# A fused two-block network on one core: the sums of the later modulation vectors streamed through columns of ones, two vectors at a time

## The reference

```python
cond = jax.nn.silu(c)                                   # (1, 1024)
for i in range(2):
    mod = (cond @ ada_w[i] + ada_b[i])[:, None, :]       # (1, 1, 6144)
    sh1, sc1, g1, sh2, sc2, g2 = jnp.split(mod, 6, axis=-1)
    h = rmsnorm(x, norm1_g[i]) * (1.0 + sc1) + sh1
    y = attention_i(h)                                   # 0: sliding window with sinks, 1: stick breaking
    x = x + g1 * y
    h = rmsnorm(x, norm2_g[i]) * (1.0 + sc2) + sh2
    x = x + g2 * swiglu(h, w_gate[i], w_up[i], w_down[i])
# then one hybrid mixer (gated convolution and SSD scan), a convolutional MLP, a last rmsnorm
```

## Time and profile before

| | us |
|---|---|
| median of 3 runs | 2310.65 (2310.07 to 2312.83) |
| the profiled execution | 2311.6 |
| its span, first to last instruction | 2309.8 |
| TensorE busy in the span | 2261.5 |
| DVE busy | 1168.9 |
| ACT busy | 883.7 |

### The profile page before, as it was taken

One profiled execution on the slowest core, in us unless ns is written; L12 is line 12 of the kernel. 1 busy time (PEld: TensorE's weight loads), 2 busy tenths in 40 slices (PEclk: granted clock), 3 DMA queues, 4 the chain that ended last, 5 costly groups with the idle time before them and its releaser, 6 DMA issues.

```text
span 2309.8 us, 27339 instructions
## 1 busy us (share of the span) xinstructions
PE 2261.5 (98%) x11136; PEld 1823.2 (79%) x11136; DVE 1168.9 (51%) x1619; ACT 883.7 (38%) x1422; POOL 165.0 (7%) x145
## 2 busy tenths in 40 slices
PE   7999999999999999999999999999999999999998
PEld 4777788888767677888887878887788887888886
DVE  4764755543455654333335446467753345553453
ACT  3654322232354543222233226467653223332331
POOL 2112000000100010000001001032120001000001
PEclk9999999999999999999999999999999999999999
DMA  9332555622212122222222223433223232323322
GB/s 343 129 108 93 190 214 199 218 101 96 78 66 72 46 74 82 99 93 100 93 99 82 100 92 111 138 105 117 98 92 128 92 101 82 100 83 109 101 82 83
DMA packets 82173, 259.13 MB, mean 112 GB/s; under 512 B 8800, under 2 KB 17248, under 8 KB 82048
## 3 DMA queue, kind: packets, MB, share of 16 engines
q1 hardware_dynamic: 82048, 257.38, 32.2%
HBM read 253.09 MB, written 4.26 MB: 111 GB/s over the span
## 4 chain that ended last, share of the span: by engine, by line
PE 93%; DVE 3%; ACT 1%; issue 1%; POOL 1%; DMA 0%; DVEq 0%; POOLq 0%; SPq 0%; ACTq 0%
PE pb L803 27%; PE pb L807 27%; PE pb L805 27%; PE pb L1015 1%; PE pb L1040 1%; PE pb L1025 1%; PE pb L848 1%; PE pb L1100 1%; PE pb L823 1%; PE pb L897 1%; PE pb L827 1%; PE pb L825 1%; PE pb L991 1%; DVE slab L1720 1%; PE pb L1106 0%
## 5 line engine op out<-in xcount | busy, mean ns | idle before, releaser
L803 PE MATMUL pb<-hhi,whi 128*128 128x512 f32 x1976 | 783.2, 396 | 4.6 <-ACT hhi L1185 3.0
L805 PE MATMUL pb<-hhi,wlo 128*128 128x512 f32 x1976 | 770.2, 390 | 2.3 <-DVE wlo L1449 2.3
L807 PE MATMUL pb<-hlo,whi 128*128 128x512 f32 x1976 | 771.0, 390 | 0.0
L1449 DVE TENSOR_TENSOR wlo<-raw,whi 128x1024 fp32r<-128x1024 f32 x361 | 447.7, 1245 | 570.0 <-ACT whi L1157 569.8
L1157 ACT ACTIVATE whi<-raw 128x1024 fp32r<-128x1024 f32 x361 | 380.2, 1057 | 730.7 <-PE pb L807 711.8
L803 PEld LDWEIGHTS pb<-hhi,whi 128*128 128x128 f32 x1976 | 370.7, 188 | 92.1 <-issue 17.8
L805 PEld LDWEIGHTS pb<-hhi,wlo 128*128 128x128 f32 x1976 | 371.1, 188 | 80.8 <-DVE wlo L1449 3.1
L807 PEld LDWEIGHTS pb<-hlo,whi 128*128 128x128 f32 x1976 | 370.6, 188 | 80.9 <-DVE hlo L1524 1.1
L803 PE MATMUL pb<-ahi,whi 128*128 128x512 f32 x848 | 334.9, 395 | 1.4 <-ACT ahi L1336 0.7
L807 PE MATMUL pb<-alo,whi 128*128 128x512 f32 x848 | 330.9, 390 | 0.0
L805 PE MATMUL pb<-ahi,wlo 128*128 128x512 f32 x848 | 330.5, 390 | 0.0
(11 more groups left out here) (234 smaller groups left out, 1676.1 us busy)
## 6 DMA issues: line engine op xcount, KB each, us to landing
raw<-stream SPq DMA_DIRECT2D x361, 512.0 KB, 3.2
slab<-ada_w SPq DMA_DIRECT2D x80, 512.0 KB, 4.8
early<-ada_w SPq DMA_DIRECT2D x32, 256.0 KB, 8.1
slab<-sums SPq DMA_DIRECT2D x32, 256.0 KB, 4.1
X<-xT SPq DMA_DIRECT2D x8, 256.0 KB, 4.9
ya<-slab SPq DMA_DIRECT2D x8, 256.0 KB, 3.5
slab<-ya SPq DMA_DIRECT2D x8, 256.0 KB, 5.1
outT<-X SPq DMA_DIRECT2D x8, 256.0 KB, 2.1
```

Source lines behind the costliest of these rows:

```text
L803: e.matmul(out, wh, hi, start=s.k == 0, stop=False)
L805: e.matmul(out, wl, hi, start=False, stop=False)
L807: i = e.matmul(out, wh, lo, start=False, stop=s.last)
L1449: e.tensor_tensor(wlo[:, u % NW, :], raw[:, u % NRAW, :], whi[:, u % NW, :].bitcast(F), ALU.subtract).then_inc(*v_cut.up(u))
```

## The change

The column sums of an accumulator go the other way round. A column of ones, repeated to 32 columns, is the stationary side, and the accumulator streams through it in two halves of 512, each into 32 partitions of one bank. Two accumulators (js) can stand side by side, in 64 partitions each. ACT copies the bank to SBUF (`modrows`), TensorE turns four pieces of up to 128 columns (`modturn`), and DVE takes one column of each 32 and adds the bias (`modadd`). Copy, turn and add come 4, 8 and 10 products behind the sums. There are six such groups instead of ten blocks: (2), (3,4), (5), (6,7), (8,9), (10,11). The group of j = 3 moves to where j = 4 stood; the pairs of the FFN stand one step behind the last accumulation of the pair, in a step of their own; (10,11) stands inside the FFN.

```diff
+    def column_sums(*js):
+        tick("modsum", js)
+        s.soon(3, "modrows", js)
+        s.soon(7, "modturn", js)
+        s.soon(9, "modadd", js)
+
     def mods():
         for j in range(2, 12):
             for k in range(KD):
-                if k == 3 and j not in (2, 5):
-                    tick("modsum", j - 1)
+                if k == 3 and j in (3, 6):
+                    column_sums(j - 1)
                 tick("fma", 8 * j + k)
                 yield 1
+            if j in (7, 9, 11):
+                column_sums(j - 1, j)
+                yield 1
...
         run(woven(some(steps, 8), some_mods(2), 3))
-        tick("modsum", 4)
+        column_sums(3, 4)
         run(steps)
...
     ffn(0, 1)
-    run(mod)
-    tick("modsum", 11)
+    assert next(mod, None) is None
...
-        def modsum(j):
-            l, jj = MODS[j]
-            b = take(("mod", j))
-            w.wait_ge(d_in, "vec")
-            w.wait_ge(v_mod, ("fma", 8 * j + 7))
-            for d in range(8):
-                i = e.matmul(b[:, d:d + 1], modacc[j % 2][:, quarter(d)], C("one"), start=d == 0, stop=True, skip_group_check=True)
-            i.then_inc(*t_mod.up(j))
-            give(("mod", j), v_mod, ("add", j))
+        def modsum(js):
+            b = take(("mod", js))
+            for n, j in enumerate(js):
+                w.wait_ge(v_mod, ("fma", 8 * j + 7))
+                for half in range(2):
+                    g = 64 * n + 32 * half
+                    i = e.matmul(b[g:g + 32, :], C("one").to_broadcast([P, 32]), modacc[j % 2][:, S * half:S * half + S], start=True, stop=True,
+                                 skip_group_check=True)
+            i.then_inc(*t_mod.up(*js))
+            give(("mod", js), a_att, ("modrows", js))
+
+        def modturn(js):
+            b = take(("columns", js))
+            n = slice(0, 64 * len(js))
+            w.wait_ge(a_att, ("modrows", js))
+            for d in range(4):
+                i = e.transpose(b[:, P * d:P * d + 64 * len(js)], sums_at(js)[n, quarter(d)], ident[n, n])
+            i.then_inc(*t_mod.up(("columns", js)))
+            give(("columns", js), v_mod, ("add", js[-1]))
...
+    def sums_at(js):
+        return slot(46) if js[-1] <= 4 else slot(16)
...
+        def modrows(js):
+            n = slice(0, 64 * len(js))
+            w.wait_ge(t_mod, js[-1])
+            e.activation(sums_at(js)[n, :], bank(("mod", js))[n, :], ACT.Copy).then_inc(*a_att.up(("modrows", js)))
...
-        def modsum(j):
+        def modadd(js):
+            for n, j in enumerate(js):
+                add_bias(js, n, j)
+
+        def add_bias(js, n, j):
             l, jj = MODS[j]
-            w.wait_ge(t_mod, j)
+            w.wait_ge(t_mod, ("columns", js))
             w.wait_ge(d_in, "vec")
             plain = jj not in (1, 4)
-            e.tensor_tensor(mod[l, jj], bank(("mod", j))[:, 0:8], W("ada_b", 48 * l + 8 * jj, 8), ALU.add).then_inc(
+            halves = lambda ap: ap.rearrange("p (h d) -> p h d", h=2)
+            sums = bank(("columns", js)).rearrange("p (d g r) -> p g d r", d=4, g=4)[:, 2 * n:2 * n + 2, :, 0]
+            e.tensor_tensor(halves(mod[l, jj]), sums, halves(W("ada_b", 48 * l + 8 * jj, 8)), ALU.add).then_inc(
```

More of the change, by code:

```diff
@@ L1109, in output @@
             give(("y", g, j), v_ssd, ("y", g, j))
-        do = {"mm": mm, "mr": mr, "evac": evac, "modsum": modsum, "pre": pre, "premod": premod, "total": total, "warm": warm, "spread": spread, "norm": norm,
+        do = {"mm": mm, "mr": mr, "evac": evac, "modsum": modsum, "modturn": modturn, "pre": pre, "premod": premod, "total": total, "warm": warm, "spread": spread, "norm": norm,
               "tables": tables, "kstat": lambda: head_stats("k"),
@@ L1418, in scalar @@
         e.activation(condp.rearrange("p (k m) -> p k m", m=32)[:, 0:8, 0:1], W("c", 0, 8).unsqueeze(2), ACT.Silu).then_inc(*a_att.up("cond"))
-        do = {"cut": cut, "sq": sq, "norm": norm, "gnorm": gnorm, "rows": rows, "sines": sines, "tables": tables, "evac": evac, "exps": exps, "turned": turned, "values": values,
+        do = {"cut": cut, "sq": sq, "norm": norm, "gnorm": gnorm, "rows": rows, "modrows": modrows, "sines": sines, "tables": tables, "evac": evac, "exps": exps, "turned": turned, "values": values,
               "vturn": vturn, "start": start, "turn": turn, "gather": gather, "dtturn": dtturn, "gsq": gsq, "xsilu": xsilu, "bturn": bturn,
@@ L1808, in vector @@
         w.wait_ge(d_in, "vec")
-        do = {"lower": lower_weights, "sq": sq, "fma": fma, "modsum": modsum, "premod": premod, "scaled": scaled, "norm": norm, "gnorm": gnorm, "final": final,
+        do = {"lower": lower_weights, "sq": sq, "fma": fma, "modadd": modadd, "premod": premod, "scaled": scaled, "norm": norm, "gnorm": gnorm, "final": final,
               "evac": evac, "kstat": lambda: head_stats("k"), "krope": lambda: rope("k"), "kspread": kspread, "query": query, "scores": scores,
```

## The result

The changed kernel took 2300.16 us (median of five runs, 2298.39 to 2301.04) where the kernel before took 2310.65 (five runs, 2310.07 to 2314.42): a ratio of 0.9945, interval 0.9934 to 0.9956, 12.7 us less (10.2 to 15.2). Forecast were 9.6 us and 2301.0. The profiled spans are 2309.8 and 2298.3.

A forecast was written before the change was run, and what follows sets the result against it. TensorE, busy 98% of the span, was taken as the bound. Terms 0.1 + 3.9 + 1.8 + 0.7 + 0.5 + 2.3 + 0.3 = 9.6 us off the 2310.65 median gave 2301.0, range 2298.5 to 2307.

The forecast's parts named there:

- The FFN term, 5.8: FFN: the single j = 5 gains 0.1 us, pairs (6,7) and (8,9) 3.9, pair (10,11) 1.8.
- The reading of the rounds of four from `pre`: New sums: passes overlap across four column groups, 0.43 us a round; two rounds cost 1.21, pair or single.
- j = 3 ... I take 2.3: Attention: taking the block at 171.26 away ends DVE's stand and frees TensorE's bank sooner, 2.3 us, ends 0 and 3.4.
- j = 2 ... Sum 0.5: Attention, block at 109: sums gain 0.6 us, the bias add costs 0.1; 0.5 in all, ends 0 and 0.7.
- their 0.45 hides in TensorE's waiting: Attention, 124 to 150: the transposes of j = 2 are covered by ACT and DVE's chain; uncovered they cost 0.45 us.
- j = 4, now (3,4) ... 0.3: Attention: two rounds of j = 3 run inside TensorE's 1.24 us wait; 1.1 and 0.45 replace 1.9, gaining 0.3.
- The clock in that norm ... I take the 0.7: Norm ahead of layer 1: the low clock goes with the one-column block, gaining 0.7 us, ends 0 and 1.4.
- Rival two: Norms: the low clock comes in other norms, 0.7 us not gained and two norms lose 0.7 each: 2303.2; chance 0.09.
- Attention gives nothing: Attention: ACT and DVE hold the joints, so its 3.1 us is not gained: 2304.1; chance 0.20.
- Calls one behind the other: New sums: column groups do not overlap, a pair costs 4.24 us, a single 2.52: 2311.3; chance 0.05.
- Transposes that wait for ACT's copy: All six groups: products queue behind transposes waiting for the copy; 3 us each would give 2319; chance 0.06.
- A one-column pass that is all but free: Old blocks: ten would cost only 4.4 us against 10.0 for six new sums: 2316; chance 0.02.

The follow-up runs named there:

- e1: Changed kernel with the new sums in the FFN alone, old blocks kept for j = 2, 3 and 4: 2306.88 us, ratio 0.9979 to the kernel before.
- e6: Changed kernel with the FFN's accumulators summed one at a time, not in pairs: 2305.94 us, ratio 0.9971 to the kernel before.
- e3: Kernel before with only the old block of j = 3 moved to right ahead of that of j = 4: 2309.32 us, ratio 0.9991.
- e11: Kernel before, unchanged, profiled once more: one run, 2313.8 us.
- e5: Changed kernel measured again, compared with the kernel before: 2301.04 us, ratio 0.9952.
- e7: Changed kernel with the pair (3,4) called four products later: 2298.22 us, ratio 0.9942 to the kernel before.
- e4: Kernel before with only the old block of j = 11 moved from ahead of layer 1's norm into the FFN: 2310.59 us, ratio 0.9996.
- e9: Kernel before with only the old block of j = 4 moved four products later: 2308.39 us, ratio 0.9984.
- e2: Changed kernel with the new sums in attention alone, old blocks kept for j = 5 to 11: 2306.74 us, ratio 0.9978 to the kernel before.
- e8: Changed kernel with the sums of j = 2 eleven products later, copy at once: 2297.11 us, ratio 0.9941 to the kernel before.

## Why the prediction came out as it did

The sign and the mechanism of the FFN and of j = 3 were right, and 2300.16 lies 0.8 us from 2301.0. But the gain was 12.7 and 11.1 us in two comparisons where 9.6 was forecast, and 12.7 lies past the 12.15 that the prediction's low end, 2298.5, allows. That low end adds the upper ends of j = 2, j = 3 and the clock; (3,4), the term that was most too small, has no end at all. The step that failed is the reading of the wait at j = 4: one profile's 1.24 us was taken for the wait of the program, and the term was put at 0.3; in most profiles of the old order the wait is 2.31 or 2.32, with a low clock behind it, and the term is 2.0 to 3.6. The terms for j = 2 and for the norm's clock failed too, the other way, and it is luck that they made up for part of it.

**The FFN term, 5.8, was right.** Six blocks of 1.81 and one of 1.72 became one single of 1.79 and three pairs of 1.20 + 0.44: 12.6 less 6.7 is 5.9, which is also what the stretches give (369.8 - 365.6 and 9.43 - 7.71). By time e1 gave 4.9 (2.8 to 6.9). The reading of the rounds of four from `pre` is what carried it, and e6 shows it from the other side.

**"j = 3 ... I take 2.3" was right.** Products 74 to 96 take 47.9 in the old order where the clock held and 45.5 in the new one, 2.4; e3 gave 2.1 by time (0.2 to 4.2). The gain isn't taken back at the next joint. The 5.33 between the two profiles first read is something else on top, a clock that fell. Stretches of e11 and then of the changed kernel:
```profile
150.00:155.00 5.00, 4.79 (x23) 3.79 (x24) 2.36 (x10) 0.00 (x0) 0.00 (x0) 0.66 0.71 251
175.00:180.00 5.00, 5.00 (x37) 4.34 (x38) 0.60 (x4) 0.78 (x2) 0.00 (x0) 0.50 0.34 105
```
```profile
150.00:155.00 5.00, 4.96 (x34) 3.53 (x34) 2.42 (x11) 1.10 (x2) 0.00 (x0) 1.00 0.66 222
175.00:180.00 5.00, 4.20 (x34) 2.95 (x33) 4.20 (x16) 4.88 (x13) 0.00 (x0) 1.00 0.00 1
```
Two of the five profiles with block 3 in its place (before and e11) have both falls, and take 50.8 and 52.3 where the others take 47.9. The fall at 150 alone came in e3 too, and with the new sums in e5 and e7, which lose 1.6 by it. So the fall at 150 doesn't come from the old block; that at 175 was seen in two of five profiles with it and in none of eight without. What decides either was not found.

**"j = 2 ... Sum 0.5" failed: it lost 0.2.** The sums gave the 0.70 (forecast 0.6). But the step "their 0.45 hides in TensorE's waiting" was wrong: the transposes stand between two products that don't wait, and cost 0.60 at this size. And "the copy just fits" was not quite so: the query products start 0.19 later behind the last product, and their first group takes 0.10 more (0.91 for 0.81). 0.6 and 0.3 are the -0.91 of the stretch from 66 to 74; with the 0.70 it makes -0.2.

**"j = 4, now (3,4) ... 0.3" is the step that failed most.** It took the 1.24 us of one profile for the wait, and no fall of the clock behind it. Of the four profiles with the old blocks 3 and 4 in their places (before, e11, e4, e1) one has that wait. In the other three POOL is served first, TensorE stands 2.31 or 2.32, and the clock falls behind it. Where DVE is served first in both, the change gives 25.73 - 25.34 = 0.4, as forecast. Where POOL is, it gives 28.4 to 30.0 less 26.4: 2.0 to 3.6. In the new order the sums of j = 3 fill part of the stand, and the granted clock stays at 1.00. e9 shows what the wait is worth without any new sums.

**"The clock in that norm ... I take the 0.7" was not shown.** The clock fell there in the profile before, but held in e2, e3, e9 and e11 with block 11 in its place. One in five with the block and none of the eight without: the block alone doesn't bring it, and the term should have stood near 0.1.

**Rival two, the low clock in other norms instead, is not refuted.** The time behind layer 1's first product is the same in the two profiles first read within 0.3, but that is a sum. From the last product ahead of a norm to the first behind it, the norm ahead of the second FFN takes 8.62 before and 7.70 after, and the two later norms with products behind them 7.61 and 7.55 before and 8.11 and 8.06 after; the longer ones have a granted clock of 0.80 or 0.81, the shorter ones 1.00. Those last two norms are long in seven of fourteen cases with the new sums in the FFN, and in one of twelve with the old. All the time behind layer 1's first product is 1695.0 with the new and 1694.4 with the old in the mean: a loss of 0.6, if it isn't chance. No run settles that.

**The sum again**, from the rows: FFN 5.8, j = 3 2.4, j = 2 -0.2, (3,4) 2.0 to 3.6, the norm's clock 0.1: 10.1 to 11.7, more where the old order meets the low clock at 150 and 175, and 0.6 less if rival two's norms belong to the change. This agrees with 11.1 and 12.7 within their intervals.

**The other rivals.** Attention gives nothing: refuted by e2, 5.1 us. Calls one behind the other: refuted by e6 and by the 0.99 of eight passes. Transposes that wait for ACT's copy: in the view of L867 TensorE sat idle ahead of it for "issue" alone, 0.7 us at two times, with no ACT in it, for all six groups. A one-column pass that is all but free: refuted already by the earlier trace rows, and here by the 1.72 that the removal of one block gives.

## What to carry to other kernels

Fewer and wider passes pay where they fill column groups that would run empty; one accumulator at a time gives nothing (1.79 against 1.81), and two are no pair if a wait stands between them (e7). Ask of a small block what stands in order behind it on the other engines: a block moved without saving a pass was worth about 2 us (e3; 0.2 to 4.2), and four products between an accumulation and its sums 3.7 (e9; 1.6 to 5.8). Take a wait from more than one profile when its releaser shares something with another engine: here a few nanoseconds of order doubled it.

## What the hardware showed that was not expected

An accumulation on DVE with both inputs in SBUF (1.28 us) and an addition on POOL that reads SBUF (1.27) do not run side by side. One runs at once. The other shows about the time of both: 2.35 to 2.38 for the accumulation, 2.40 for the addition, and 3.57 for the addition in e2 and e8, where DVE's next instruction (1.22) went ahead of it too. Their order changed between two profiles of one program (before and e11). The Trainium skill's page "SBUF — State Buffer", section "SBUF: two separate sides", says that the two engines share a pair of ports as an exclusive lock, held for a whole instruction by whoever comes first. This case's traces agree on the lock: the 70 accumulations of each of the thirteen profiles show 1.25 to 1.29 or 2.35 to 2.38, and never a value between. Who came first they can't tell at the pair (3,4): the recorded starts lie within 4 ns of each other, and in five of the ten profiles in which POOL ran at once DVE's start is recorded 1 or 2 ns ahead.

What follows is larger than the lock itself. The extra 1.07 us of DVE made TensorE stand 2.31 instead of 1.24, and behind the longer stand it ran at the 1.2 GHz level for a while (matmuls 0.43 apart), so that the stretch lost 28.44 - 25.73 = 2.7 us in e11 and 30.00 - 25.73 = 4.3 in e1, where the 16 passes themselves show 3.39 us instead of 1.92. Timeline of TensorE in e1:
```profile
209.88 3.39 PE L858 MATMUL pb<-cst,slab 128*128 128x1 f32 x16 [2.32 <-DVE slab L1506]
```
That holds for all three profiles with the stand of 2.31 or 2.32 (e11, e4, e1). But a long stand isn't the only way: in e3 the clock fell behind block 3's sixteen passes and a stand of 0.64. It was not tried to take POOL's addition away from that moment.
